# One encoder layer on one core: kept gate groups, shorter norms, and gates and a token projection moved to the softmax

## What is computed

```
proj = x @ w_in                       # q, k, v | hq, hf, hi, hg | ga, gh
attn = sliding_window_gqa_sinks(...)  # chunks of 64, window of 2 chunks, softmax with sinks
rec  = hgrn2(...)                     # 4 heads, chunked recurrence, RMS norm, silu gate
mixed = sigmoid(ga) * (attn @ w_proj_attn) + sigmoid(gh) * (rec @ w_proj_hgrn)
x = layer_norm(ALPHA * x + mixed @ w_out)
# PEER: 8 heads, 2 x 128 keys, top 16 of the pairs, 128 of 16384 experts per token
hid = u[e] . x ;  out = sum_k softmax(score)_k * gelu(hid_k) * v[e_k]
x = layer_norm(ALPHA * x + out)
```

## Time and profile before

| what | value |
|---|---|
| median of 3 runs | 1640.93 us (1637.55 to 1645.9) |
| the profiled execution | 1638.83 us, span in the trace 1636.8 us, mean granted clock 0.965 |
| busy, PE / PE weight loads | 1536.4 us (94%) / 1093.9 us (67%) |
| busy, DVE / ACT / POOL | 1126.5 us (69%) / 272.9 us (17%) / 611.6 us (37%) |
| transfers | 540.77 MB, mean 330 GB/s |
| stores of gate groups | 8 of 2048 KB |
| loads of gate blocks | 16 of 1024 KB |
| loads of u blocks, v blocks | 128 and 128 of 512 KB |
| stores and loads of activations | 12 and 12 of 1024 KB |

### The profile page before, as it was taken

One profiled execution on the slowest core, in us unless ns is written; L12 is line 12 of the kernel. 1 busy time (PEld: TensorE's weight loads), 2 busy tenths in 40 slices (PEclk: granted clock), 3 DMA queues, 4 the chain that ended last, 5 costly groups with the idle time before them and its releaser, 6 DMA issues.

```text
span 1636.8 us, 17961 instructions
## 1 busy us (share of the span) xinstructions
PE 1536.4 (94%) x6542; PEld 1093.9 (67%) x6542; DVE 1126.5 (69%) x2364; ACT 272.9 (17%) x543; POOL 611.6 (37%) x516
## 2 busy tenths in 40 slices
PE   7798998789998799999999999999789999999997
PEld 7697777565557566788889999998534444444443
DVE  1414799987769999999967889898644534444443
ACT  2601213621010111111123333432000000000000
POOL 0000543466667473322324555556533323232100
PEclk9899998879999799999999999999899999999999
DMA  7586967777999797898888999999999999999962
GB/s 289 209 276 215 399 225 267 255 244 265 413 405 372 270 409 284 313 328 301 316 289 298 413 412 414 411 385 397 404 400 371 381 383 375 391 379 386 365 206 103
DMA packets 146663, 540.77 MB, mean 330 GB/s; under 512 B 14992, under 2 KB 34192, under 8 KB 134032
## 3 DMA queue, kind: packets, MB, share of 16 engines
q0 software_dynamic: 73728, 268.47, 43.8%
q1 hardware_dynamic: 71696, 254.38, 41.6%
q10 hardware_dynamic: 1152, 16.78, 2.4%
HBM read 508.11 MB, written 31.46 MB: 330 GB/s over the span
## 4 chain that ended last, share of the span: by engine, by line
PE 76%; DVE 12%; DMA 6%; issue 3%; ACT 2%; SPq 1%; POOL 0%; DVEq 0%
PE bank L834 26%; PE bank L859 25%; PE bank L739 7%; PE bank L814 6%; PE bank L852 3%; DVE arena L1160 2%; DMA arena<-v_cols_d 2%; DVE arena L1175 2%; PE bank L774 2%; PE bank L749 1%; DMA arena<-gates_d 1%; PE bank L751 1%; PE bank L586 1%; DMA arena<-w_items_d 1%; DMA arena<-u_d,arena 1%
## 5 line engine op out<-in xcount | busy, mean ns | idle before, releaser
L1589 POOL DMA_INDIRECT arena<-u_d,arena x256 | 334.2, 1305 | 501.8 <-DVE arena L1160 254.5
L859 PE MATMUL bank<-arena 128*128 128x512 f32 x1024 | 444.5, 597 | 17.4 <-DVE arena L1498 12.1
L834 PE MATMUL bank<-arena 128*128 128x256 f32 x2048 | 453.8, 381 | 3.6 <-DMA arena<-u_cols_d 3.6
L1589 POOL DMA_INDIRECT arena<-v_d,arena x256 | 277.2, 1083 | 419.3 <-DVE arena L1175 357.2
L834 PEld LDWEIGHTS bank<-arena 128*128 128x128 f32 x2048 | 386.2, 191 | 53.6 <-issue 3.8
L859 PEld LDWEIGHTS bank<-arena 128*128 128x128 f32 x1024 | 196.1, 192 | 265.4 <-issue 245.1
L1175 DVE SCALAR_TENSOR_TENSOR arena<-arena 128x1024 f32<-128x1024 f32 x256 | 327.6, 1280 | 11.0 <-DMA arena<-v_d,arena 3.0
L1160 DVE CUSTOM_DVE_ANT_0 arena<-arena 128x1024 f32<-128x1024 f32 x256 | 304.3, 1220 | 30.5 <-DMA arena<-u_d,arena 29.7
L1498 DVE TENSOR_TENSOR arena<-arena 128x256 f32<-128x256 f32 x128 | 53.2, 419 | 216.6 <-DMA arena<-act_d 177.7
L814 PE MATMUL bank<-arena 128*128 128x128 f32 (+1 forms) x512 | 118.1, 392 | 1.4 <-ACT arena L1020 1.4
L739 PE MATMUL bank<-arena 128*128 128x128 f32 (+1 forms) x512 | 113.8, 384 | 0.2 <-DMA arena<-w_items_d 0.2
(11 more groups left out here) (199 smaller groups left out, 1072.9 us busy)
## 6 DMA issues: line engine op xcount, KB each, us to landing
arena<-w_items_d SPq DMA_DIRECT2D x66, 1024.0 KB, 7.3
arena<-u_cols_d SPq DMA_DIRECT2D x128, 512.0 KB, 7.0
arena<-v_cols_d SPq DMA_DIRECT2D x128, 512.0 KB, 7.3
gates_d<-arena ACTq DMA_DIRECT2D x8, 2048.0 KB, 11.9
arena<-gates_d SPq DMA_DIRECT2D x16, 1024.0 KB, 11.2
act_d<-arena SPq DMA_DIRECT2D x12, 1024.0 KB, 9.3
arena<-act_d SPq DMA_DIRECT2D x12, 1024.0 KB, 13.0
arena<-u_d,arena POOLq DMA_INDIRECT x256, 8.9
```

Source lines behind the costliest of these rows:

```text
L834: last = mm(bank[:, 4 + c % 2, 0:ND], u_buf[:, c % UBUFS, k, :], B.act_in[:, k, B.n - ND:B.n], start=k == 0, stop=k == KC - 1)
L859: last = mm(bank[:, 2 * n + half, :], act_slot(i)[:, n * P:(n + 1) * P], v_buf[i % VBUFS][:, half * 512:(half + 1) * 512], start=i == 0, s ...
L1589: pool.indirect_dma_start(rows[:, r % SLOTS, :], None, table, bass.IndirectOffsetOnAxis(eidx[:, t, k:k + 1], 0)).then_inc(landed[r % SLOTS ...
```

## The change

- **Kept gate groups.** The last two of eight groups (`STORED = GROUPS - 2`) are not stored; they stay in the two staging buffers, and `weigh` multiplies 192 columns from the loaded block and 64 from the kept groups, in two instructions. The gate blocks loaded are 768 KB instead of 1024 KB.
- **More v buffers.** Eight instead of six, partly in memory that the u blocks and one-hot matrices leave.
- **Norms.** The mean is subtracted and the gain applied in one pass that doesn't need the root; the second pass scales and adds the bias, in two halves that are announced singly. In the output projection the statistics of a half are taken as soon as it is there.
- **Output projection.** The products of the first seven c blocks of the first units (two in A, four in B) run before the last mix. The row schedule of DVE there is other (`AT_OUT`, `OUT_STEP`).
- **Front B.** Token projection 5 goes between score chunks 3 and 4; gates 0 and 1 go ahead of and behind the first two transposes of softmax weights, into banks 0 to 3; ACT copies all token projections before it normalises, and takes the four sigmoids before the copies of the transposed keys.
- **Schedule.** Spreading runs over blocks 53 to 116, with 104 rows beside it.
- **The end.** The last four blocks are summed by tile and half, and the norm and stores follow by halves.

```diff
-UBUFS, VBUFS = 4, 6
+UBUFS, VBUFS = 4, 8
...
+STORED = GROUPS - 2
...
-SPREAD_AT, SPREAD_END = 56, 114
+SPREAD_AT, SPREAD_END = 53, 116
...
-HOT_ROWS = 96
+HOT_ROWS = 104
...
-ODD_STEP, AT_OUT, OUT_STEP, HGRN_STEP, STATE_STEP = 5, 152, 9, 3, 2
+ODD_STEP, AT_OUT, OUT_STEP, HGRN_STEP, STATE_STEP = 5, 148, 2, 3, 2
...
-        v_buf = [view(kb, D) for kb in (140, 144, 64, 68, 72, 76)]
+        v_buf = [view(kb, D) for kb in (172, 176, 164, 168, 48, 52, 56, 60)]
...
-        stage = [view(148, EXPERTS, GROUP), view(64, EXPERTS, GROUP)]
-        g_buf = [view(148 + 8 * k, GROUPS, GBLK, GROUP) for k in range(2)]
+        stage = [view(64, EXPERTS, GROUP), view(148, EXPERTS, GROUP)]
+        g_buf = [view(kb, STORED, GBLK, GROUP) for kb in (140, 104)]
+
+        g_kept = view(0, 2, 84 * KB)[:, :, 64 * KB:80 * KB].rearrange("p g (e t) -> p g e t", t=GROUP)
...
+        def gate_bank(F, m):
+
+            return 2 * m if F is B and m < 2 else 4 * (m % 2)
...
-            sp.wait_ge(idx_ready, 2 * PH)
+            sp.wait_ge(pick_ready, len(DENSE))
             for i in range(2):
                 load_v(i)
             for k in range(2):
-                sp.wait_ge(g_stored[k], 16 * (GROUPS // 2))
+                sp.wait_ge(g_stored[k], 16 * (STORED // 2))
             load_gates(0)
-            for i in range(2, VBUFS):
+            sp.wait_ge(g_done, QUADS)
+            for i in range(2, 4):
+                load_v(i)
+            for i in range(4, VBUFS):
+                sp.wait_ge(h_done, EXPERTS + i + 1 - VBUFS)
...
                     if c >= 4:
+                        if c == 4:
+                            project_tok(TOK_EARLY)
                         pe.wait_ge(F.score_out, c - 3)
...
-                for k in range(TOK_EARLY, N_TOK):
+                for k in range(TOK_EARLY + (F.nc > 4), N_TOK):
...
+                def gates(m):
+                    k = I_MIX + 3 * (m // 2) + m % 2
+                    item_in(pe, F, k)
+                    w = item(F, k).rearrange("p (c n) -> p c n", n=P)
+                    if m >= 2:
+                        pe.wait_ge(F.mix_out, m - 1)
+                    elif F is B:
+                        pe.wait_ge(F.proj_out, 2 * N_HQF + N_TOK * nt)
...
+                    b = gate_bank(F, m)
...
+                if F is B:
+                    gates(0)
                 pe.wait_ge(F.reached, V_ZERO)
                 turn_weights(0)
+                turn_weights(1)
+                if F is B:
+                    gates(1)
                 for c in range(F.nc):
-                    if c + 1 < F.nc:
+                    if 0 < c < F.nc - 1:
                         turn_weights(c + 1)
                     times_v(c)
...
-                pe.wait_ge(F.proj_out, 2 * N_HQF + N_TOK * nt)
+                if F is B:
+                    pe.wait_ge(F.gate_ready, 4)
+                else:
+                    pe.wait_ge(F.proj_out, 2 * N_HQF + N_TOK * nt)
...
-                    gates(m)
-                    gates(m + 1)
+                    if m or F is A:
+                        gates(m)
+                        gates(m + 1)
...
+                def sum_out(u, c):
+                    k, t = out_units(F)[u]
+                    w = item(F, I_OUT + k).rearrange("p (c n) -> p c n", c=KC)
+                    return mm(bank[:, u % 4, 0:TW], F.mixT[:, c, t * P:(t + 1) * P], w[:, c, :],
+                              start=c == 0, stop=c == KC - 1)
+
+
+                begun = 2 if nt == 1 else 4
+                pe.wait_ge(F.mix_out, KC - 1)
+                for u in range(begun):
+                    item_in(pe, F, I_OUT + out_units(F)[u][0])
+                    for c in range(KC - 1):
+                        sum_out(u, c)
                 pe.wait_ge(F.mix_out, KC)
                 for u, (k, t) in enumerate(out_units(F)):
                     item_in(pe, F, I_OUT + k)
-                    w = item(F, I_OUT + k).rearrange("p (c n) -> p c n", c=KC)
                     if u >= 4:
                         pe.wait_ge(F.y_out, u - 3)
-                    for c in range(KC):
-                        last = mm(bank[:, u % 4, 0:TW], F.mixT[:, c, t * P:(t + 1) * P], w[:, c, :],
-                                  start=c == 0, stop=c == KC - 1)
+                    for c in range(KC - 1 if u < begun else 0, KC):
+                        last = sum_out(u, c)
...
+                for n in range(len(DENSE)):
+                    for half in range(2):
+                        for i in range(EXPERTS - LAST, EXPERTS):
+                            if n == half == 0:
+                                pe.wait_ge(w_ready, i + 1)
+                                pe.wait_ge(v_in[i % VBUFS], 16 * (i // VBUFS + 1))
+                            last = sums(i, n, half)
+                        last.then_inc(o_done, 1)
...
+                if F is B:
+                    for k in range(TOK_EARLY + 1, N_TOK):
+                        copy_tok(k)
...
+                def gate_sigmoids(m):
+                    act.wait_ge(F.gate_done, m + 1)
+                    if m >= 2:
+                        act.wait_ge(F.mix_out, m - 1)
+                    for k in range(2):
+                        fn(F.sig[:, m % 2, k, :], bank[:, gate_bank(F, m) + k, 0:n], ACT.Sigmoid).then_inc(F.gate_ready, 1)
...
+                if F is B:
+                    gate_sigmoids(0)
+                    gate_sigmoids(1)
...
-                if k == GROUP // QUAD - 1:
+                if k == GROUP // QUAD - 1 and g < STORED:
...
-                    if t == 0 and k < N_OUT - 1:
-                        rows_until(AT_OUT + OUT_STEP * k)
+                    rows_until(AT_OUT + OUT_STEP * min(u, F.nt * (N_OUT - 2)))
...
+                    if k >= N_OUT - 2:
+                        dve.wait_ge(F.y_out, u + 1)
+                        half_stats(F.x1[:, t, :], k - (N_OUT - 2))
                     if k == N_OUT - 1:
-                        dve.wait_ge(F.y_out, u + 1)
-                        layer_norm(t, F.x1[:, t, :], F.x1[:, t, :], F.var_ready, F.std_ready, F.x1_ready)
-
-            def norm_stats(src, var_ready):
-
-                for n in range(2):
-                    ch(v.bn_stats(stats[:, n, :], src[:, n * 512:(n + 1) * 512]))
+                        norm_var(F.var_ready)
+                        norm_scale(t, F.x1[:, t, :], F.std_ready, F.x1_ready)
...
-            def norm_scale(t, src, dst, std_ready, ready):
-
+            def norm_scale(t, y, std_ready, ready):
+
+                steps(lambda: v.scalar_tensor_tensor(out=y, in0=y, scalar=mv[:, 0:1], in1=ln_gb[:, 0, :],
+                                                     op0=ALU.subtract, op1=ALU.mult))
                 dve.wait_ge(std_ready, t + 1)
                 steps(lambda: v.reciprocal(rstd[:, :], rstd[:, :]))
-                steps(lambda: v.tensor_scalar(dst, src, mv[:, 0:1], rstd[:, 0:1], ALU.subtract, ALU.mult))
-                steps(lambda: v.tensor_tensor(dst, dst, ln_gb[:, 0, :], ALU.mult))
-                v.tensor_tensor(dst, dst, ln_gb[:, 1, :], ALU.add).then_inc(ready, 1)
-                dve.wait_ge(ready, t + 1)
-
-            def layer_norm(t, src, dst, var_ready, std_ready, ready):
-
-                norm_stats(src, var_ready)
-                norm_scale(t, src, dst, std_ready, ready)
+                for half in range(2):
+                    part = slice(512 * half, 512 * half + 512)
+                    v.scalar_tensor_tensor(out=y[:, part], in0=y[:, part], scalar=rstd[:, 0:1], in1=ln_gb[:, 1, part],
+                                           op0=ALU.mult, op1=ALU.add).then_inc(ready, 1)
+                dve.wait_ge(ready, 2 * t + 2)
...
-                v.tensor_tensor(a, a, g_buf[b % 2][:, :, i % GBLK, :], ALU.mult).then_inc(w_ready, 1)
...
+                v.tensor_tensor(a[:, 0:STORED, :], a[:, 0:STORED, :], g_buf[b % 2][:, :, i % GBLK, :], ALU.mult)
+                v.tensor_tensor(a[:, STORED:GROUPS, :], a[:, STORED:GROUPS, :], g_kept[:, :, chunk(i), :],
+                                ALU.mult).then_inc(w_ready, 1)
...
+            dve.wait_ge(g_out, QUADS)
```

99 lines of the change are left out of this document (46 added, 53 removed).

## The result

The changed kernel took 1632.42 us (median of 20 runs, 1621.71 to 1640.85); the kernel before, on the same chip, 1640.93 us (20 runs, 1636.54 to 1649.31). The ratio is 0.994, with an interval from 0.992 to 0.9959: 8.5 us less. I had forecast 1620, 21 us less. The sign was right and 1632 lies in the range, but the gain is less than half of the forecast.

The account below looks back on a forecast made before the run. PE was taken to carry the span, with DVE nearly full up to the picks. Terms of -7.4 (up to the picks), -10.0 (step) and -2.7 (end) took 1638.83 to 1618.7; with the median 2.1 above, 1620 us, range 1603 to 1634.

Parts of the forecast that it names:

- The execution it was read from: Whole kernel: terms were taken from one profiled execution of 1638.83 us, the median of the runs 2.1 us above it.
- the hoist: Front B softmax pause: token projection (10.3 us) fills PE's 5.06 us wait, then PE pauses about 10 us; alone +2.8 us.
- pushes the last two score chunks back by some 5 us, to about 296: Front B scores behind the early token projection: DVE asks for them only then, so the delay loses nothing.
- Nothing of the 20.6 us that moved is gained: +2.7 us.: Front B, moved gates 0 and 1: gates 2 start at 405.4 instead of 402.61; between -3 and +6 us.
- Front A, -4.5 us.: Front A's norm: products before the last mix, shorter norm and restart save 4.5 us, between 3 and 6.5.
- Output and norm of B, 17.2 us for PE.: Front B's output projection: half of the last tile is there at 542.0 instead of 559.26, 17.2 us for PE.
- The picks as the cap.: Transposes ahead of block 52: DVE ready at 833.9, PE at 825.0; 8.9 us stop and half-clock restart leave 7.4 of 19 us.
- The step to combining, -10.0 us.: Hidden blocks to combining: first wait 3.0 us shorter, v waits (5.3) and second restart (1.7) go; between 0 and -17.
- Rival (b): Step to combining gains nothing: queues full, neither the wait nor v waits shrink; 1629 us, chance 0.18.
- (a): Rival: DVE reaches the picks with PE, or the gate block is issued earlier, wait about 4 us; about 1606, chance 0.22.
- (c): Rival: DVE drops rows in front B's longer attention chain, debt lasts to the picks, queues slow spreading; 1655 us, chance 0.10.
- The end, -2.7 us.: After the last sum: norm by halves leaves 4.6 us instead of 7.3.

Follow-up runs that it names:

- e1: The kernel before, unaltered, run and profiled a second time: 1654.45 us.
- s1: Changed kernel with only token projection 5 put back behind all front B scores, row gathers not paced: 1623.56 us, ratio 0.9881.
- a1: The changed kernel, unaltered, run for a second profile: 1632.84 us, ratio 0.9931.
- h1: The changed kernel, unaltered, run again on another chip: 1632.67 us, ratio 0.9894.
- o1: Changed kernel with row gathers 1 to 4 paced and token projection 5 back behind all scores, gates 0 and 1 still moved: 1622.74 us.
- m1: Changed kernel with GpSimd's row gathers 1 to 4 paced, one for each of front A's heads 5 to 8: 1626.13 us.
- b1: Changed kernel with front B's gates 0 and 1, token projection 5 and ACT's order put back as in the kernel before: 1627.29 us, ratio 0.9887.
- q1: Changed kernel with row gathers paced, token projection 5 back behind all scores, and picks three blocks later: 1612.77 us, ratio 0.9814.
- r1: Changed kernel with row gathers paced, token projection 5 back behind all scores, 8 DVE row operations moved behind the picks: 1619.43 us.
- g1: Changed kernel with front B's gates 0 and 1, token projection 5 and ACT's order put back, and picks three blocks later: 1634.4 us.
- j1: Changed kernel with row gathers paced and front B's gates 0 and 1, token projection 5 and ACT's order put back: 1626.04 us.
- p1: As j1, with the rotation of front B's heads done one head of picks earlier (`ROPE_HEAD` 6 to 5): 1626.81 us.
- d1: Kernel before with only the kept gate groups, eight v buffers and the split multiply: 1636.09 us, ratio 0.9943.
- k1: Changed kernel with 8 of DVE's row operations moved from ahead of the gate arguments to behind the picks: 1633.37 us.
- f1: Changed kernel with no row gathered until front A's query projections are out: 1639.17 us, ratio 0.9936.

## Why the prediction was right and wrong

- **The execution it was read from.** This step failed first, and it carries most of the miss. "The profiled execution took 1638.83 us ...; the median of the runs is 2.1 us above it": close in time, but not alike inside. That execution had no stutter, and the prediction has no term for one. All nine later profiles with the gathers as they were have it, in e1 worth 14.8 us at front B's first scores (288.15 for 273.33). The waits of 5.06 and 2.89 us in the earlier trace rows, which the hoist was to fill, are absent in such an execution; e1 has neither. The changed kernel's median lies 10.1 us over its first profile, not 2.1: 8.0 of the 12.4 us that are missing. How much of this is a stutter that the changed kernel has more often, and how much the tile that makes one dearer, stays open.
- **"... pushes the last two score chunks back by some 5 us, to about 296. DVE asks for them only then, so nothing is lost."** This is the step of the sum that failed. Counted from front B's first scores, the exponentials begin 27.4 us later in the first profile of the kernel before and 28.7 us in that of the changed one, so in such an execution the hoist costs 1.4 us there and VectorE's date nearly covers it. With a stutter it is 17.9 us in e1 and 17.7 in s1, but 27.1 in a1 and h1: 9.2 us, nearly the whole tile (10.3 us), are on the path. The second half of the step, the pause of 10 us behind it, was right in eight profiles (9.96 to 10.00 us). Priced at +2.8 us, the tile costs 3.4 us on one chip with pacing (o1 against m1), and 9 us without it by medians of different chips (s1).
- **"Nothing of the 20.6 us that moved is gained: +2.7 us."** Together 5.5 us (b1). The gates by themselves seem to gain: from the exponentials to the first output product it takes 196.3 to 199.2 us in the four profiles with only the gates moved (o1, q1, r1, s1), and 200.4 to 202.8 in the four with both back (b1, g1, j1, p1). The times don't settle it: s1 lies 3.7 us under b1, but on another chip, and their ratios are 0.9881 and 0.9887.
- **Front A, -4.5 us.** The first transposes come 2.9 us earlier in the first profile, and 1.8 us in a1 against e1, which ran on different chips. The wait for the norm is 3.96 us for 6.18, a saving of 2.2 where 2.5 was forecast. A wait of 1.0 us for weights at the last output units took the place of the 0.97 us that went, and nothing of the 1.0 us for a shorter restart shows at the transposes.
- **Output and norm of B, 17.2 us for PE.** Right. From the first output product to the last tile's transposes before 58.7 us, after 46.4 us, and the 4.89 us wait ahead of it is gone: 17.2.
- **The picks as the cap.** Right in kind: new waits for VectorE of 5.86 us, and 8.0 to 12.68 us in the versions where PE is early (b1, o1, s1). Picks three blocks later then gave 10.0 us (o1 to q1, on two chips; s1 to q1 on one chip is 10.8, the pacing included). The cost of the wait was priced at 8.9 us and the restart; it was 5.86 us in the first profile, because PE came to the hidden blocks 11.0 us later than forecast and the picks were ready only 6.5 us later. In the usual execution of the changed kernel the cap hardly binds (1.83 us in a1, none in h1), because PE lost the time before.
- **The step to combining, -10.0 us.** 7.7 by d1. The wait fell from 12.06 to 8.76 us and the 5.3 us of v waits went. Rival (b), that the step gains nothing, is refuted. Of (a) its first half came true by another road: in h1 PE doesn't wait for the picks at all, but because it is late itself, so nothing was gained. (c) didn't occur: no debt of rows, the stretch from the picks to combining lasted 329.4 to 331.7 us in the three profiles of the changed kernel (332.5 before).
- **The end, -2.7 us.** From PE's last sum to the end of the execution 12.4 us before, 9.2 after: 3.2.
- **The sum.** 1618.7 and the 2.1 us make 1620.8; the forecast says 1620.

So by the medians of the chip where the parts were measured, 9 us of the forecast 20 are missing: 2.3 at the step, 4.0 in the rest and 2.8 in the moved work. In the first comparison the gain was 2.5 us smaller still, no more than the medians of the kernel before differ by chip (1639 to 1650 us). These are differences of medians that may mix executions with and without a stutter; they say which edit the loss hangs on, not how it comes about.

## What to carry to other kernels

Before costing a pause from one profile, take a second one of the same kernel: a pause that a late engine closes is not there to be filled. Work hoisted into a pause should be something whose successor is also free; here it stood ahead of two small score chunks for which two engines waited. And when a gain upstream vanishes, look for the next engine's date (here VectorE's picks) and move blocks ahead of it: picks three blocks later gave some 10 us where PE was early (q1), and fewer rows ahead of the picks nothing where PE was late itself (k1).

## What the runs showed of the hardware

- PE can fall to about one matmul record per 0.7 us (1.4 in e1) with no cause in the profile while indirect gathers fill the queues (390 to 414 GB/s, share 0.99 to 1.02 in the nine profiles; 412 and 1.02 in a1), and the granted clock then goes to the 1.2 GHz level (0.50 in a1 from 172 to 182 us). With the gathers paced (360 to 381 GB/s, 0.93 to 0.98) or held (288 GB/s, 0.83) it was gone from front A in all nine profiles; in front B's key scores, where nothing is held, f1 still has 8.5 us of it. Full queues are not enough: the first profile of before had 406 GB/s and share 1.00 without it. The Trainium skill ("Runtime: NRT & Kernel Launch", Instruction fetch mechanics) says that instructions come in 16 KB blocks over a queue of their own, at a cost mostly hidden. The page of the profile has that queue (52 packets, 0.85 MB), and in a1, e1 and s1 no packet of it moves between 160 and 188 us, where the first profile of before has one at 176 to 180. That fits a late block, but not matmuls that trickle on at 0.7 us, and the profile doesn't say which engine a packet is for; the cause was only argued, and what the runs show is the dependence on the gathers.
- The same instructions in one kernel differed by 15 us at one place between executions, and by 11 us in the median between chips; the changed kernel's medians agreed within 0.5 us on three.
